# Attention bias moved from VectorE into a TensorE accumulation, and three steps of the layer plan moved one weight unit later

## The chip, the cores and the metric

The kernel runs on one NeuronCore of one Trainium2 chip. The metric is the device time of one execution in microseconds (us). TensorE (PE) does matrix products into PSUM; VectorE (DVE) and ScalarE (ACT) work on SBUF and PSUM; GpSimd (POOL) does some elementwise work; SyncE (SP) issues the loads. Each engine takes its own instructions in order and waits for the others on semaphores.

## What is computed

The reference is a trunk of two equal layers on 256 tokens of width 1024. Each layer mixes tokens in three branches and then runs a SwiGLU feed-forward. The branch that the change touches most is the differential attention (8 heads, two score maps each). Its bias is minus a slope of the head times the distance of query and key:

```python
def block(args):
    qi, start = args
    sc = jnp.einsum('bqhcd,bkhcd->bhcqk', qi, k, preferred_element_type=jnp.float32)
    qpos = start + jnp.arange(Q_BLOCK)
    dist = jnp.abs(qpos[:, None] - kpos[None, :]).astype(jnp.float32)
    sc = sc - slopes[None, :, None, None, None] * dist
    p = jax.nn.softmax(sc, axis=-1)
    attn = p[:, :, 0] - lam * p[:, :, 1]
    return jnp.einsum('bhqk,bkhe->bqhe', attn.astype(v.dtype), v)
...
cb = jnp.einsum('bclgn,bcsgn->bcgls', Cc, Bc)
m = cb[:, :, :, None] * segsum_exp(a)
y_diag = jnp.einsum('bcgrls,bcsgrp->bclgrp', m, xdt)
```

The last three lines belong to the state-space branch (32 heads in 4 groups, 2 chunks of 128 tokens, forwards and backwards); `cb` is the product of its C and B rows. The third branch attends to a memory (4 heads). The branches are gated and projected (`w_branch`, `w_out`).

## The kernel before, in words

**Units.** All weights of a layer are cut into 220 units of 512 KB. Per unit SP loads the raw fp32 weights, ACT casts them to fp32r (`wH`, `split_h`, L818), DVE or POOL subtracts to get the rest (`wL`, `split_l`, L1163 and L1093), and PE multiplies three times (high by high, low by high, high by low), 24 matmuls of 256 columns or 12 of 512. There is a ring of 4 slots. ACT, DVE and SP work 3 units ahead of PE: what these engines do "after unit u" comes behind their part for unit u + 3. Units come in groups of 4 to 11 that share a PSUM pair; after the last unit of a group ACT or DVE empties it.

**Steps.** Everything that is not a unit is a step. `layer_plan` (L107 to L196) writes down after which unit a step stands, and all engines walk the same list in `each_step` (L404): unit, emptying of a finished group, steps. So the order on every engine is fixed, and an engine that waits in a step holds all that stands behind it. In a layer the units are: 26 to 49 the q, k, v projections, 50 to 73 the inputs of the state-space branch (`xbc`), 74 to 89 its gate `z`, 90 to 121 gates and projections of two branches, 122 to 145 gate and projection of the state-space branch, then the output projection and the feed-forward (154 on). The numbers are those of the plan before the change.

**Attention.** A head is four steps. `da_scores`: PE makes both score maps in the side banks S0 and S1; DVE adds the distances times -8 slope while copying to `sc` (L1362), takes the row maximum (L1365) and its negative (L1367); ACT takes the exponential in place with row sums (L954). `da_combine`, two units later: DVE joins the maps (L1371 to L1379). `da_turn`: PE transposes the result into S2 (L695), ACT copies it to `attT` (L959). `da_values`, one unit later: PE multiplies by v, ACT scales and squares (L967, L972). Heads 0 to 3 begin every 3 units (from unit 39), heads 4 to 7 every 4 units (from unit 54). Beside heads 4 to 7 runs the convolution on DVE (`conv`, L1401 and L1407), two steps of about 4.6 us for every 4 units, followed by its silu on ACT (L984) and transposes (`xs_turn`).

**State-space branch.** `cb_diag` after unit 77: DVE multiplies B by C (`cbprod`, L1429), PE sums it in 8 one-column matmuls into S2; `d_gain` (DVE, L1434) uses them. `cb` of group 0 is after unit 77 as well; it needs the last silu. From there a pipeline of 16 ticks runs to unit 123: `rows` (SP loads rows), `diff` (DVE, L1447, L1449), `decay_exp` (ACT, L1014), `decay` (DVE, L1457), `diag` and `off` (PE), `assemble` (DVE, L1467 to L1479), `ssm_norm`, `ssm_out` (PE transposes, L776, then DVE L1492, ACT L1027, DVE L1170). The last four `ssm_out` stand after units 125 to 128; unit 130 on PE waits for the last of them (L1499).

## Time and profile before

| | |
|---|---|
| median of three timed runs | 1583.02 us (1580.55, 1583.02, 1587.58) |
| the profiled execution | 1577.17 us, its span 1575.4 us |
| PE busy | 1437.5 us, 91% of the span |
| DVE busy | 983.2 us, 62% |
| ACT busy | 803.5 us, 51% |
| mean granted TensorE clock | 0.973 |
| chain that ended last | PE 57%, DVE 15%, the sequencer of DVE (DVEq) 9%, ACT 8%, issue 6% |
| read from memory | 252.80 MB, 161 GB/s over the span |

Busy time is the time in which an instruction runs; short matmuls overlap, so a matmul of 512 columns lasts about 0.4 us and the next one starts after 0.23 us. DVEq rows are drains, in which the engine empties its pipeline; they are not counted as busy. The two layers give the same rows some 771 us apart. All times of rows below are in us from the start of the span, durations by group in ns.

### The profile page before, as it was taken

To read this page: it belongs to the slowest core of one execution; us is meant where nothing else is said; L and a number is where in the kernel's file an instruction comes from. 1 tells how busy PE (TensorE), PEld (TensorE's weight loads), DVE (VectorE), ACT (ScalarE), POOL (GpSimd) and SP (SyncE) were. 2 spreads that over 40 slices of the span, in tenths; PEclk is the share of its full clock that TensorE was granted. 3 is DMA by queue.
4 is the path that set the end of the run, shared out by engine and by line. 5 is a ranking of instruction groups with operands and counts; after the bars stand their busy time and mean duration, and the time that the engine had idled before them with its cause. 6 is when DMAs were issued, how large, how long until landed. Compare 5 with 4: busy or idle time off the path is not lost.

```text
span 1575.4 us, 25511 instructions
## 1 busy us (share of the span) xinstructions
PE 1437.5 (91%) x8889; PEld 1280.5 (81%) x8889; DVE 983.2 (62%) x1288; ACT 803.5 (51%) x1151; POOL 338.5 (21%) x162
## 2 busy tenths in 40 slices
PE   5999887969898999999999998886998899999997
PEld 4899787858677779999889987786886677799986
DVE  5445569977787635555432555799677775465544
ACT  4545556746343545444444555675554344454453
POOL 2410000001112144454433000000011113345453
PEclk9999999989999999999999999999899999999999
DMA  5644343455654555656555444335655555565664
GB/s 191 196 144 127 118 121 107 135 149 199 203 150 155 165 172 161 196 168 227 189 170 178 134 124 120 108 110 150 194 190 164 157 161 176 159 187 174 196 215 149
DMA packets 158499, 255.52 MB, mean 162 GB/s; under 512 B 12730, under 2 KB 58924, under 8 KB 158380
## 3 DMA queue, kind: packets, MB, share of 16 engines
q1 hardware_dynamic: 156427, 252.41, 51.6%
q10 hardware_dynamic: 1952, 1.61, 0.3%
q8 instruction: 64, 1.05, 0.3%
q14 instruction: 56, 0.45, 0.1%
HBM read 252.80 MB, written 1.18 MB: 161 GB/s over the span
## 4 chain that ended last, share of the span: by engine, by line
PE 57%; DVE 15%; DVEq 9%; ACT 8%; issue 6%; DMA 2%; ACTq 1%; SPq 0%; POOL 0%; POOLq 0%
PE PS L528 52%; ACT wH L818 4%; DVE wL L1163 4%; PE S L528 4%; DVE regA L1407 3%; DVEq L1404 3%; DMA w_raw<-in_w_branch_dram 2%; DVEq L1448 1%; DVE small L1365 1%; ACT scr L954 1%; DVEq L1364 1%; PE S L535 1%; DVE scr L1449 1%; DMA w_raw<-in_w_in_dram 1%; ACT regA L984 1%
## 5 line engine op out<-in xcount | busy, mean ns | idle before, releaser
L1163 DVE TENSOR_TENSOR wL<-w_raw,wH 128x1024 fp32r<-128x1024 f32 (+1 forms) x330 | 461.3, 1404 | 391.6 <-ACT wH L818 378.1
L818 ACT CAST wH<-w_raw 128x1024 fp32r<-128x1024 f32 (+1 forms) x443 | 455.0, 1041 | 239.9 <-PE PS L528 201.4
L528 PE MATMUL PS<-hH,wH 128*128 128x256 f32 x1472 | 424.6, 288 | 0.0
L528 PE MATMUL PS<-hL,wH 128*128 128x256 f32 x1472 | 418.9, 285 | 0.0
L528 PE MATMUL PS<-hH,wL 128*128 128x256 f32 x1472 | 418.8, 285 | 0.0
L1093 POOL TENSOR_TENSOR wL<-w_raw,wH 128x1024 fp32r<-128x1024 f32 (+1 forms) x113 | 286.0, 2533 | 433.7 <-ACT wH L818 433.6
L528 PEld LDWEIGHTS PS<-hH,wH 128*128 128x128 f32 x1472 | 285.1, 194 | 5.0 <-issue 4.6
L528 PEld LDWEIGHTS PS<-hL,wH 128*128 128x128 f32 x1472 | 285.1, 194 | 0.3
L528 PEld LDWEIGHTS PS<-hH,wL 128*128 128x128 f32 x1472 | 284.7, 193 | 0.0
L528 PE MATMUL PS<-wH,actH 128*128 128x512 f32 x560 | 223.8, 400 | 3.1 <-DVEq L1499 3.1
L528 PE MATMUL PS<-wH,actL 128*128 128x512 f32 x560 | 219.6, 392 | 0.0
L528 PE MATMUL PS<-wL,actH 128*128 128x512 f32 x560 | 219.5, 392 | 0.0
L528 PE MATMUL PS<-wH,hH 128*128 128x512 f32 (+1 forms) x416 | 167.6, 403 | 1.7 <-DVE wL L1163 1.7
L528 PE MATMUL PS<-wL,hH 128*128 128x512 f32 (+1 forms) x416 | 161.8, 389 | 0.0
L528 PE MATMUL PS<-wH,hL 128*128 128x512 f32 (+1 forms) x416 | 161.8, 389 | 0.0
L1109 POOL TENSOR_TENSOR scr<-regA,dts 128x512 f32<-128x512 f32 x16 | 21.7, 1359 | 603.8 <-DVEq L1409 472.4
L528 PEld LDWEIGHTS PS<-wH,actH 128*128 128x128 f32 x560 | 106.2, 190 | 24.8 <-DVEq L1499 3.9
L528 PEld LDWEIGHTS PS<-wL,actH 128*128 128x128 f32 x560 | 106.0, 189 | 22.9
L528 PEld LDWEIGHTS PS<-wH,actL 128*128 128x128 f32 x560 | 106.2, 190 | 20.7
L528 PEld LDWEIGHTS PS<-wH,hH 128*128 128x128 f32 x416 | 81.1, 195 | 19.2 <-DVE wL L1163 3.4
L528 PEld LDWEIGHTS PS<-wL,hH 128*128 128x128 f32 x416 | 80.7, 194 | 16.2
L528 PEld LDWEIGHTS PS<-wH,hL 128*128 128x128 f32 x416 | 80.8, 194 | 14.3
(223 smaller groups left out, 1510.4 us busy)
## 6 DMA issues: line engine op xcount, KB each, us to landing
w_raw<-in_w_in_dram SPq DMA_DIRECT2D x192, 512.0 KB
w_raw<-in_w_ffn_in_dram SPq DMA_DIRECT2D x176, 256.0 KB
w_raw<-in_w_branch_dram SPq DMA_DIRECT2D x64, 512.0 KB
w_raw<-in_w_ffn_out_dram SPq DMA_DIRECT2D x44, 512.0 KB
w_raw<-in_w_mem_kv_dram SPq DMA_DIRECT2D x35, 512.0 KB
scr<-cs_rows SPq DMA_DIRECT2D x64, 256.0 KB, 5.1
w_raw<-in_w_out_dram SPq DMA_DIRECT2D x16, 512.0 KB
regA<-in_mem_dram SPq DMA_DIRECT2D x6, 512.0 KB, 4.8
```

Source lines behind the costliest of these rows:

```text
L528: return nc.tensor.matmul(o, l, r, start=first, stop=last, skip_group_check=True)
L535: ins = nc.tensor.transpose(dst[:, at:at + P], src(t, k), ident[:, :])
L818: nc.scalar.copy(wH[:, slot].rearrange("p k c -> p (k c)")[:, q], raw[:, slot].rearrange("p k c -> p (k c)")[:, q]).then_inc(h_done[slot], 1)
L954: nc.scalar.activation(v, v, ACT.Exp, bias=nmx[b][:, q:q + 1], scale=0.125, accum_out=sm[b][:, q:q + 1])
L984: nc.scalar.activation(cacc[i % 2], cacc[i % 2], ACT.Silu)
L1093: nc.gpsimd.tensor_tensor(wL[:, slot].rearrange("p k c -> p (k c)")[:, q], raw[:, slot].rearrange("p k c -> p (k c)")[:, q], wH[:, slot].r ...
L1109: nc.gpsimd.tensor_tensor(v3(xw, HPG), v3(xsN[:, 1 - c, UC * g:UC * (g + 1)], HPG), wgt[:, q:q + HPG].unsqueeze(2).broadcast_to([P, HPG, DH]),
L1163: v.tensor_tensor(wL[:, slot].rearrange("p k c -> p (k c)")[:, q], raw[:, slot].rearrange("p k c -> p (k c)")[:, q], wH[:, slot].rearrange ...
L1364: dve.drain()
L1365: v.tensor_reduce(mx[b], v3(sc[b], 4), AX.X, ALU.max)
L1404: dve.drain()
L1407: v.scalar_tensor_tensor(cacc[b % 2][:, j, :], cin[:, j, k:k + T], p_cw[:, q:q + 1], cacc[b % 2][:, j, :], ALU.mult, ALU.add)
```

## The change

Four things are changed. (1) The bias: for each map PE first multiplies a constant tile `slopes` (a diagonal of -8 slope, bf16) by `dist` into S0 or S1 (128x512) and then adds the scores onto it. DVE takes the maximum straight from the two banks, one reduction each; the addition L1362 is gone. ACT takes the exponential from the banks into `sc` and now frees them; it also writes the tile for the head after next (`slope_tile`). (2) `da_turn` and `da_values` of every head stand one unit later. (3) `cb_diag` becomes two steps, `cb_prod` on DVE and `cb_diag` on PE a unit later; `d_gain` stands after unit 81 in place of 78. (4) All ticks, with `cb`, `rows`, `ssm_norm` and `ssm_out`, stand one unit later.

```diff
@@ layer_plan
         put(at, "da_scores", h)
         put(at + 2, "da_combine", h)
-        put(at + 3 + (h >= HALF), "da_turn", h)
-        put(at + 4 + (h >= HALF), "da_values", h)
+        put(at + 4 + (h >= HALF), "da_turn", h)
+        put(at + 5 + (h >= HALF), "da_values", h)
...
-    start, per = u + 5, 1.28
-    put(u + 3, "cb_diag", 0)
-    put(u + 4, "d_gain", 0)
+    start, per = u + 6, 1.28
+    put(u + 4, "cb_prod", 0)
+    put(u + 5, "cb_diag", 0)
+    put(u + 7, "d_gain", 0)
@@ PE, da_scores
                         take(lay, m)
+                        if m == 0:
+                            pe.wait_ge(slope_ready, HEADS * lay + i + 1)
+                        mm(S[m][:, :], slopes[:, P * (i % 2):P * (i % 2 + 1)], dist[:, :], True, False)
                         r = slice(DH * m, DH * (m + 1))
                         for t in range(NT):
                             ins = mm(S[m][:, T * t:T * (t + 1)], qT[half][r, j, P * t:P * (t + 1)],
-                                     kT[half][r, j, :], True, True)
+                                     kT[half][r, j, :], False, True)
@@ ACT
+            def slope_tile(i):
+                nc.scalar.activation(slopes[:, P * (i % 2):P * (i % 2 + 1)], ident[:, :], ACT.Copy,
+                                     scale=-8.0 * slope(i)).then_inc(slope_ready, 1)
...
                 elif kind == "da_scores":
                     b = i % 2
+                    if i >= 2:
+                        act.wait_ge(da_turned, HEADS * lay + i - 1)
+                    else:
+                        act.wait_ge(xa_turned, XH * lay + XH)
                     act.wait_ge(da_max, HEADS * lay + i + 1)
                     for q in range(4):
-                        v = sc[b][:, T * q:T * (q + 1)]
-                        nc.scalar.activation(v, v, ACT.Exp, bias=nmx[b][:, q:q + 1], scale=0.125,
-                                             accum_out=sm[b][:, q:q + 1])
+                        ins = nc.scalar.activation(sc[b][:, T * q:T * (q + 1)],
+                                                   S[q // 2][:, T * (q % 2):T * (q % 2 + 1)], ACT.Exp,
+                                                   bias=nmx[b][:, q:q + 1], scale=0.125,
+                                                   accum_out=sm[b][:, q:q + 1])
+                        if q % 2 == 1:
+                            ins.then_inc(side_free[q // 2], 1)
+                    if i + 2 < HEADS:
+                        slope_tile(i + 2)
                     act.drain().then_inc(da_exp, 1)
@@ DVE
                 elif kind == "da_scores":
                     b = i % 2
                     dve.wait_ge(da_sc, HEADS * lay + i + 1)
-                    if i >= 2:
-                        dve.wait_ge(da_turned, HEADS * lay + i - 1)
-                    else:
-                        dve.wait_ge(xa_turned, XH * lay + XH)
                     for m in range(2):
-
-                        v.scalar_tensor_tensor(sc[b][:, 512 * m:512 * (m + 1)], dist[:, :], -8.0 * slope(i),
-                                               S[m][:, :], ALU.mult, ALU.add).then_inc(side_free[m], 1)
-                    dve.drain()
-                    v.tensor_reduce(mx[b], v3(sc[b], 4), AX.X, ALU.max)
+                        v.tensor_reduce(mx[b][:, 2 * m:2 * m + 2], v3(S[m][:, :], 2), AX.X, ALU.max)
                     dve.drain()
...
-                elif kind == "cb_diag":
+                elif kind == "cb_prod":
                     dve.wait_ge(silu_done, 6 * lay + 6)
                     dve.wait_ge(da_yt, 4 * lay + 4)
                     v.tensor_tensor(cbprod, BT, CT, ALU.mult).then_inc(prod_done, 1)
```

The order on ACT around head 1 (`regB<-PS` copies empty groups, `scr<-S` by a COPY is the turned map going to `attT`, the four ACTIVATE are the exponentials). Before:

```order
L818 CAST wH<-w_raw 128x1024
L959 COPY scr<-S 128x512
L951 REGISTER_ALU
L954 ACTIVATE scr,small<-scr,small 128x256 x4
L818 CAST wH<-w_raw 128x1024
L967 ACTIVATE scr<-S,small 128x128 x2
L972 ACTIVATE junk,small<-scr 128x128 x2
```

After (L824 is the cast, L971 the exponentials, L912 the slope tile, L982 the copy of the turned map, L990 and L995 the values):

```order
L824 CAST wH<-w_raw 128x1024
L969 REGISTER_ALU
L971 ACTIVATE scr,small<-S,small 128x256 x4
L912 ACTIVATE slopes<-ident 128x128
L824 CAST wH<-w_raw 128x1024
L982 COPY scr<-S 128x512
L824 CAST wH<-w_raw 128x1024
L990 ACTIVATE scr<-S,small 128x128 x2
L995 ACTIVATE junk,small<-scr 128x128 x2
```

The copy of the turned map of head 0 stood before the exponentials of head 1 and now stands behind them, the slope tile and one more cast.

The order on PE after the last attention transposes (L712), where `onesR,scr` are the one-column sums of `cbprod` and `regA` by `regA` is `cb`. Before:

```order
L712 MATMUL S<-ident,scr 128x128 x4
L524 REGISTER_ALU
L528 MATMUL S<-onesR,scr 128x1 x8
L524 REGISTER_ALU
L749 REGISTER_ALU
L528 MATMUL S<-regA 128x256 x2
L590 REGISTER_ALU
L528 MATMUL PS<-wH,hH 128x512
```

After, with the 12 matmuls of unit 79 ahead of the first row:

```order
L531 MATMUL PS<-wL,hH 128x512
L527 REGISTER_ALU
L531 MATMUL S<-onesR,scr 128x1 x8
L595 REGISTER_ALU
L531 MATMUL PS<-wH,hH 128x512
```

The sums now stand behind units 78 and 79, and `cb` between these two.

On DVE at the same place (L1171 is the low part of the last attention output, L1429 `cbprod`, L1447 and L1449 `diff`). Before:

```order
L1171 SCALAR_TENSOR_TENSOR actL<-S,lp,actH 128x512
L1427 ISA
L1429 TENSOR_TENSOR scr<-regA 128x1024
L1446 REGISTER_ALU
L1447 TENSOR_TENSOR scr<-scr,dts 128x512
```

After:

```order
L1194 SCALAR_TENSOR_TENSOR actL<-S,lp,actH 128x512
L1186 TENSOR_TENSOR wL<-w_raw,wH 128x1024
L1442 ISA
L1444 TENSOR_TENSOR scr<-regA 128x1024
L1461 REGISTER_ALU
L1462 TENSOR_TENSOR scr<-scr,dts 128x512
```

One split of weights more stands ahead of `cbprod` and of `diff`.

## Rows read from the trace of the kernel before

**Rows 1.** Windows: stretch, its length, busy of PE PEld DVE ACT POOL, clock, DMA

```profile
160.00:222.00 62.00, 53.63 (x394) 48.85 (x392) 33.77 (x49) 36.11 (x82) 0.00 (x0) 1.00 0.41 120
222.00:323.00 101.00, 85.47 (x628) 78.67 (x624) 92.80 (x172) 66.47 (x114) 0.00 (x0) 0.97 0.43 125
333.00:340.00 7.00, 6.79 (x24) 6.14 (x25) 1.99 (x4) 1.29 (x2) 0.00 (x0) 0.52 0.38 99
340.00:410.00 70.00, 70.00 (x331) 57.52 (x329) 51.93 (x63) 40.41 (x48) 8.39 (x7) 1.00 0.59 201
410.00:534.00 124.00, 106.78 (x479) 85.12 (x478) 95.54 (x115) 53.33 (x69) 16.02 (x10) 0.94 0.53 158
```

**Rows 2.** Waits of PE, whole span: total us, times, longest

```profile
PE S L695 <- DVEq L1379: 30.5, 14, 4.3
PE S L528 <- DVE scr L1429: 20.6, 2, 10.3
PE S L528 <- DVEq L1471: 19.5, 7, 5.0
```

**Rows 3.** Timeline, head 2 of the first layer: start, duration, engine, what

```profile
184.39 1.14 PE L528 MATMUL S<-regB 64*128 64x256 f32 x8
188.47 0.51 ACT L954 ACTIVATE scr<-scr,small 128x256 f32<-128x256 f32 x1 [3.39 <-DVE small L1367]
193.20 1.99 ACT L818 CAST wH<-w_raw 128x1024 fp32r<-128x1024 f32 x2
195.99 0.88 DVE L1377 SCALAR_TENSOR_TENSOR scr<-scr,small 128x256 f32<-128x256 f32 x2
196.95 0.66 PE L695 MATMUL S<-ident,scr 128*128 128x128 f32 x4 [2.14 <-DVEq L1379]
```

**Rows 4.** Groups of instructions by line and shape: count, busy us, mean ns

```profile
L1362 DVE SCALAR_TENSOR_TENSOR scr<-dist,S 128x512 f32<-128x512 bf16 x32 | 20.5, 682 | 3.6 <-PE S L528 3.0 <-issue 0.6
L1365 DVE TENSOR_REDUCE small<-scr 128x4 f32<-128x1024 f32 x16 | 19.5, 1220 | 1.5
L1338 DVE TENSOR_REDUCE small<-S 128x2 f32<-128x512 f32 x8 | 5.5, 692 | 6.1 <-PE S L528 6.1
L954 ACT ACTIVATE scr<-scr,small 128x256 f32<-128x256 f32 x64 | 31.8, 497 | 47.8 <-DVE small L1367 47.8
L937 ACT ACTIVATE scr<-S,small 128x256 f32<-128x256 f32 x16 | 7.4, 470 | 16.6 <-DVE small L1340 16.6
L972 ACT ACTIVATE junk<-scr 128x128 bf16<-128x128 f32 x32 | 9.6, 302 | 1.4
L528 PE MATMUL S<-scr,cboff 128*128 128x512 f32 x16 | 8.2, 592 | 0.0
```

**Rows 5.** Timeline from the last attention output to unit 78, first layer

```profile
322.24 0.66 PE L712 MATMUL S<-ident,scr 128*128 128x128 f32 x4 [1.65 <-DVE actL L1171]
326.95 1.06 ACT L984 ACTIVATE regA<-regA 128x1024 f32<-128x1024 f32 x1 [9.98 <-DVEq L1409]
331.83 1.23 DVE L1429 TENSOR_TENSOR scr<-regA 128x1024 f32<-128x1024 f32 x1 [0.28 <-issue]
333.21 3.55 PE L528 MATMUL S<-onesR,scr 128*128 128x1 f32 x16 [10.31 <-DVE scr L1429]
338.11 0.99 PE L528 MATMUL PS<-wH,hH 128*128 128x512 f32 x1
```

**Rows 6.** Timeline, last two `ssm_out` and unit 130, first layer

```profile
529.44 0.62 ACT L1027 CAST actH<-scr 128x512 fp32r<-128x512 f32 x1 [1.94 <-DVEq L1494]
532.95 0.62 ACT L1027 CAST actH<-scr 128x512 fp32r<-128x512 f32 x1 [1.94 <-DVEq L1494]
534.38 0.50 PE L528 MATMUL PS<-wH,actH 128*128 128x512 f32 x1 [1.55 <-DVEq L1499]
534.95 0.40 PE L528 MATMUL PS<-wL,actH 128*128 128x512 f32 x1
535.18 0.39 PE L528 MATMUL PS<-wH,actH 128*128 128x512 f32 x1
```

More of the change, by code:

```diff
@@ L242, in build @@
         junk = sb("junk", UC, BF16)
+        slopes = sb("slopes", 2 * P, BF16)
         def v3(ap, n):
@@ L346, in build @@
             "cst_turned", "cst_copied", "cst_stored", "dt_log"))
+        slope_ready = sem("slope_ready")
         prod_done, cbdiag_done, dgain_done = sem("cb_prod"), sem("cb_diag"), sem("d_gain")
@@ L933, in step @@
                 elif kind == "xa_scores":
+                    if i == 0:
+                        slope_tile(0)
+                        slope_tile(1)
                     b = i % 2
```

## The prediction

> **What bounds the kernel now.** I read the table of windows first, then the list of PE's waits, then the timeline at the three places where these waits are. PE is busy 91% of the span, so a change pays only where PE stands still, or where PE's wait is the end of a chain on DVE and ACT that the change makes shorter. The windows [rows 1] show three regimes in the mixing part of a layer. From 160 to 222 (heads 0 to 3) PE is busy 53.6 of 62 us, DVE only 33.8 and ACT 36.1: no engine is full, so the holes in PE are latency. From 222 to 323 (heads 4 to 7 beside the convolution) DVE is busy 92.8 of 101 us, and with its drains full; PE's 85.5 is what DVE lets through. From 340 to 410 PE is busy all the time. (A unit of 12 fp32r matmuls of 512 columns is 2.76 us of PE, 0.23 apart from start to start, 534.95 to 535.18 [rows 6]; the units of 24 with 256 columns take as long.) From 410 to 534 DVE and ACT hand work to each other and PE waits again.
>
> The waits [rows 2] say what PE stood still for: 30.5 us for the joined attention map before its transposes (14 waits in two layers, 7 per layer), 20.6 us for `cbprod` (twice 10.3), and 19.5 us in the ticks for S2 to be freed. The first two are what the change aims at. The second layer repeats the first, so I work out one layer and double it.
>
> **Heads 0 to 3: the turn a unit later.** Head 2 shows the chain [rows 3]: PE begins the scores at 184.39 and ends them at 185.5; DVE adds the bias and takes the maximum, and the exponentials start at 188.47 (four at 0.5, to 190.5); then ACT has two casts and the values of the head before between them, DVE a split of weights behind the second cast, and the join from 195.99 lets the transposes go at 196.95, after a wait of 2.14. The four heads wait 62.0 - 53.6 = 8.4 us together [rows 1]. Moved one unit, the transposes have 2.76 us more of PE work ahead of them, and also the values and scores that used to follow; the chain itself is 1.2 us shorter (next part). The mean wait is 2.1, less than the one unit, so all 8.4 go.
>
> Two things come back. First, the bias costs PE two matmuls of 128x512 per head. No bf16 matmul is in the trace. Below, it is nothing where PE would wait anyway; above, the nearest row is the fp32 one of the same shape, which comes as two instructions of 592 ns that overlap [rows 4], about 1.0 us. I take 0.23, the spacing of the fp32r matmuls of 512 columns [rows 6]. 8 matmuls are 1.8 us (range 0 to 8). The Trainium skill ("TensorE: Matmul & The Clock Gate", section "Back-to-back issue gap") gives about 216 ns for an isolated bf16 matmul of 512 columns and about 131 ns in a sustained stream; by these the 8 would be 1.7 or 1.0 us. No bf16 row here decides it, and the fp32r spacing of 230 ns stands nearer to the first.
>
> Second, a new wait. The copy of the turned map stood before the exponentials of the next head on ACT and now stands behind four exponentials, a slope tile and a cast, while PE reaches the values 2.76 us after the transposes. Counted from the end of the scores: two reductions and the negation 1.6 us, four exponentials and the sums 2.2, the slope tile 0.3 (like the small ACTIVATE of 302 ns [rows 4]), a cast 1.0 [rows 3], and, as estimates from that cast, 0.8 for a copy of half its size with its drain: 5.9 us. PE has a unit, the transposes of 0.66 and a unit, 2.76 + 0.66 + 2.76 = 6.2. That is level; semaphores add a little, and at head 2 the emptying of a group (a copy as large as a cast, 1.0 us) comes between. I take 1.6 us for the four (0 to 5).
>
> Sum on PE: 8.4 - 1.8 - 1.6 = 5.0 us. The norm of the first four heads must now wait for values that come one unit later, with a square root and a table load in front of it, and DVE stands in that norm before the maximum of head 4. I count 0.6 for it, so DVE begins the second half **4.4 us** earlier (1 to 7).
>
> **Heads 4 to 7: DVE is the bound.** Per head two additions of 682 ns go, and one reduction of 1220 ns becomes two of 692, by the reductions of memory attention from PSUM [rows 4]: 1.36 - 0.16 = 1.2 less. Four heads: **4.8 us** (4.2 to 5.5). PE's bias matmuls here lie under DVE, as do ACT's: its exponentials get 27 ns faster each (470 from PSUM against 497 [rows 4]). The turn moved later frees nothing here but PE, which then waits for DVE in another place. The Trainium skill has a rule against this edit ("VectorE: DVE Perf Modes", section "The TRN2 errata"): a PSUM source costs DVE a fixed 120 cycles, an SBUF source 58. For 512 and 1024 elements at its 0.96 GHz that is two times 658 ns in place of 1127, 0.19 us more per head where the rows make it 0.16; by it the four heads would give 4.7 us.
>
> **`cbprod`.** Before [rows 5]: the last attention transposes end at 322.90; PE waits for `cbprod` until 333.21, does the sums (3.55) and `cb` at the half clock (333 to 340 has a granted clock of 0.52 [rows 1], that is 1.2 GHz), and starts unit 78 at 338.11. Two units more, the first partly at the half clock, put unit 80 at 344.6. The stretch from 322.90 is 21.7 us. After, on the same base: unit 78 to 325.7; `cb` waits for the silu, which ends at 328.0 [rows 5], then 1.0; unit 79 to 331.9; the sums wait for `cbprod`. That ended 5.0 us after the silu; one split (1.2) is added ahead of it, so it ends near 334.3. The sums take 1.8 at the full clock: unit 80 at 336.1. That is 8.5 us less, but the ticks now hang on a unit 2.76 later: **5.7 us** for what follows. On DVE the second `diff` gives the same within 0.5. Bounds: if the clock stays low because two shorter waits stand there, 3; if ACT's cast for the split comes early, 8.
>
> **Ticks.** The plan of all ticks moves as one, with SP's `rows` loads between the same weight loads relative to the ticks, and POOL's `scale` and `off` too. The number of table switches on ACT stays. I count nothing. `d_gain`, three units later, is used first by POOL five units on. PE full from 340 to 410 means that an earlier start there is passed on.
>
> **The end of the branch.** The last four `ssm_out` are a loop of DVE and ACT with 3.51 us per turn (529.44 to 532.95 [rows 6]), and unit 130 waits 1.55 for it. All of it now stands behind one more split on DVE, 1.2 us: **-1.3 us** (0 to -2.8; the latter if the loop is paced by PE, a whole unit).
>
> **Sum.** Per layer 4.4 + 4.8 + 5.7 - 1.3 = 13.6 us, two layers 27. From the profiled 1577.2 (span 1575.4 and 1.8 around it) that is 1550. The median of the timed runs, 1583.0, is 5.8 above the profiled execution; I add it: **1556 us**, 1.7% less.
>
> **Rivals.**
>
> *The gain stops at the ticks.* From 340 on the stage is held by DVE and ACT hand-offs and by loads at 201 GB/s [rows 1]. If loads or these hand-offs take back what PE wins before, only what DVE does less stays: 4.8 + 1.2 per layer, 12 us in all, 1571 us. For it: after 410 every PE wait ends on DVE [rows 2]. Against: nothing in the stage is tied to an outside clock, DVE itself arrives earlier, and 125 GB/s before 323 leave the loads slack.
>
> *More than that.* If no new wait comes at the values (+1.6), `cbprod` gives 8 and the 19.5 us of waits for S2 [rows 2] shrink by a quarter because POOL and ACT are further ahead, it is 20 us per layer: 1543 us. For it: the waits shorten the low clock stretches as well (0.94 mean from 410 to 534 [rows 1]). Against: the order inside the ticks is unchanged.
>
> *Slower: the values wait for ACT.* PE waits at `da_values` because the copy is behind the exponentials. It is level by my sum (5.9 against 6.2). It turns the result over if it costs more than 13.6 / 8 = 1.7 us on each of eight heads beyond my count. At 3 us a head (exponentials from PSUM delayed by the maximum, plus an emptied group each time) it is 24 per layer, ten more than the gain: 1583 + 20 = 1603 us. Against: in heads 4 to 7 a wait of PE below DVE's pace is free, so only heads 0 to 3 can pay, 12 us at most; and ACT is busy 36 of 62 us. That makes it unlikely.
>
> A fourth: the bias matmul in another number format could cost 1.0 us each; 8 per layer on PE's path add 6 per layer, 1568 us. It is within the range.
>
> **How the numbers follow.** 0.62 for the forecast (own range 1548 to 1566), 0.18 for the gain that stops at the ticks, 0.12 for more, 0.04 for slower, 0.04 for no change by mishap of parts. The range must leave no more than 0.2 out: 1541 to 1572 takes in most of the first three and the bounds of the terms. A measurement of this kernel tells 0.5% (7.9 us) from no change. Below 1575: nearly all of the first three, less the upper end of the second, 0.88. Within 0.5%: 0.08. Slower: 0.04.
>
> **What would show it.** PE's wait for the join gone in heads 0 to 3 and small in heads 4 to 7; a new small PE wait for ACT's copy at the values, 0 to 1 us; the bias matmuls 0.23 apart; DVE's period per head of 4 units shorter by 1.2; in place of the 10.3 us two waits of about 2.4 at `cb` and at the sums, with the clock full soon after; unit 80 some 18 us earlier than at 344.6 (9 from upstream, 8.5 here); unit 130's wait a little longer. I am wrong if the waits in the ticks grow by what is won before, or if the wait at the values exceeds 2 us a head.

## The result, and the profile after

| | before | changed |
|---|---|---|
| median of the timed runs | 1583.42 us (4 runs, 1580.55 to 1587.58) | 1567.85 us (4 runs, 1562.98 to 1572.21) |
| profiled execution: span, time | 1575.4, 1577.17 | 1561.1, 1562.98 |
| busy PE / DVE / ACT | 1437.5 / 983.2 / 803.5 us (91% of the span for PE) | 1465.0 / 971.7 / 804.8 us (94% for PE) |

The ratio is 0.9907, 95% interval 0.9888 to 0.9925: some 15 us faster. The forecast was 1556, 27 us faster, with a range of 1541 to 1572. The sign, the place and the range were right; about half of the gain is missing.

Windows of the changed kernel, first layer, in the columns of [rows 1] (busy times in the order PE, PEld, DVE, ACT, POOL). The first goes from the scores of head 0 to just after those of head 4, the third from the last attention transposes to the end of the sums of `cbprod`:

```profile
158.00:218.00 60.00, 59.67 (x402) 52.14 (x400) 29.51 (x45) 37.83 (x86) 0.00 (x0) 1.00 0.42 123
218.00:312.00 94.00, 87.17 (x628) 80.01 (x626) 86.11 (x165) 65.57 (x116) 0.00 (x0) 0.98 0.44 129
312.00:326.00 14.00, 10.70 (x46) 8.38 (x47) 12.72 (x19) 7.05 (x8) 1.04 (x1) 0.86 0.39 115
326.00:340.00 14.00, 14.00 (x51) 11.37 (x52) 7.79 (x12) 8.73 (x9) 1.04 (x1) 0.77 0.69 226
394.00:523.00 129.00, 108.87 (x486) 86.84 (x486) 99.53 (x116) 55.86 (x73) 15.05 (x11) 0.93 0.50 155
```

Read the first row against [rows 1]: PE's holes in heads 0 to 3 are gone (59.67 of 60.00 busy, against 53.63 of 62.00), and yet the stretch is only 2 us shorter. PE waited 8.0 us less and worked 6.0 us more. That is one of the missing pieces, and the timeline of head 2 shows it. Behind the row of the scores in [rows 3], the next unit of the kernel before began here:

```profile
185.46 0.50 PE L528 MATMUL PS<-wH,hH 128*128 128x512 f32 x1
```

In the changed kernel:

```profile
179.78 0.39 PE L531 MATMUL S<-dist,slopes 128*128 128x512 bf16 x1
180.10 1.13 PE L531 MATMUL S<-regB 64*128 64x256 f32 x4
181.16 0.39 PE L531 MATMUL S<-dist,slopes 128*128 128x512 bf16 x1
181.49 1.13 PE L531 MATMUL S<-regB 64*128 64x256 f32 x4
182.54 0.50 PE L531 MATMUL PS<-wH,hH 128*128 128x512 f32 x1
```

Before, the eight score matmuls of both maps stood in one row of 1.14 us, and the next unit began 1.07 after their start (184.39 to 185.46). Now four of them, one map, take 1.13 us by themselves (1.06 to the next start), after a bias matmul that takes 0.32 to the next start. The step is 182.54 - 179.78 = 2.76 us, 1.7 longer than before; I had counted 0.46.

The waits of PE over the whole span, which answer to [rows 2]:

```profile
PE S L531 <- DVEq L1486: 25.5, 9, 6.6
PE PS L531 <- DVEq L1514: 8.6, 2, 4.3
PE S L531 <- ACTq L983: 6.7, 4, 3.0
PE S L531 <- ACTq L1008: 4.9, 2, 2.4
PE S L531 <- DVE scr L1444: 1.3, 2, 0.7
```

The 30.5 us for the join are gone, the 20.6 for `cbprod` have become 4.9 for the silu and 1.3 for `cbprod`. What grew: the ticks' wait for S2 (19.5 to 25.5), unit 130's wait (twice 4.3, where [rows 6] has 1.55), and the new wait of the values for ScalarE's copy (twice 0.33 and twice 3.04, L983 is the drain behind that copy).

Groups by line and shape, in the columns of [rows 4]:

```profile
L1380 DVE TENSOR_REDUCE small<-S 128x2 f32<-128x512 f32 x32 | 20.6, 684 | 11.9 <-PE S L531 11.9
L971 ACT ACTIVATE scr<-S,small 128x256 f32<-128x256 f32 x64 | 29.4, 472 | 46.3 <-DVE small L1382 46.3
L912 ACT ACTIVATE slopes<-ident 128x128 bf16<-128x128 f32 x16 | 4.8, 314 | 0.0
```

These are the estimates of the prediction (692, 470, 302 ns) within 4%. The `cb` stretch of the first layer, answering to [rows 5]:

```profile
312.20 0.66 PE L718 MATMUL S<-ident,scr 128*128 128x128 f32 x4 [1.63 <-DVE actL L1194]
318.03 1.50 PE L531 MATMUL S<-regA 128*128 128x256 f32 x4 [2.44 <-ACTq L1008]
324.19 2.38 PE L531 MATMUL S<-onesR,scr 128*128 128x1 f32 x16 [0.66 <-DVE scr L1444]
326.43 0.77 PE L531 MATMUL PS<-wH,hH 128*128 128x512 f32 x1
330.42 0.63 PE L531 MATMUL PS<-wH,hH 128*128 128x512 f32 x1
```

The fourth row starts unit 80, 14.2 us after the transposes; before it was 22.4 (322.24 to 344.60). The 0.63 in the last row (0.40 at the full clock) is TensorE at 1.2 GHz: the granted clock is 0.77 in the window that starts at 326. Unit 79, ahead of the sums, ran at 1.2 GHz in part as well (0.43 a matmul until 321.9).

To split the gain I cut a layer at five places that both traces have: the scores of head 0, the scores of head 4, the last attention transposes, the first `off` that reads `cboff` (the third of the layer; "the first `off`" below) and the first transposes of the feed-forward input (its row with `xN`). Starts in the first layer: 158.97, 221.16, 322.24, 395.37, 598.62 before; 155.50, 215.49, 312.20, 382.81, 590.86 after.

| stretch, first layer | before | changed | gain | forecast |
|---|---|---|---|---|
| heads 0 to 3 | 62.2 | 60.0 | 2.2 | 4.4 |
| head 4 to the last attention output | 101.1 | 96.7 | 4.4 | 4.8 |
| to the first `off` | 73.1 | 70.6 | 2.5 | 5.7 |
| to the feed-forward input | 203.2 | 208.1 | -4.8 | -1.3 |
| sum | 439.7 | 435.4 | 4.3 | 13.6 |

The second layer gives the same within 0.6 (439.1 and 435.2). The two layers account for 8 of the 14.3 us between the spans. The other 6 lie where the change does nothing: 3.4 ahead of the first layer's memory attention and 2.5 between the first layer's feed-forward input and the second layer's head 0 (331.7 and 329.2 us). For the first of these, the same window of before and, in the second fence, of the changed kernel:

```profile
97.00:104.00 7.00, 7.00 (x37) 7.00 (x37) 3.58 (x7) 3.88 (x4) 0.00 (x0) 0.53 0.54 164
```

```profile
97.00:104.00 7.00, 7.00 (x62) 7.00 (x62) 5.05 (x13) 5.90 (x8) 0.00 (x0) 1.00 0.55 153
```

The granted clock (third number from the end) is 0.53 in the one and 1.00 in the other, with no idle time in either. Over the thirteen profiles of this study that attention starts between 105.1 and 109.1 us, and the second stretch takes 329.2 to 335.4; the changed kernel's profile has the lowest of both. So a profile alone can't tell 3 us from nothing. The medians must decide, and the experiments are read by them first.

### The profile page after: what moved, and what is told of

It reads as the page before. It is cut to its first block, busy times and chain, and to the rows that moved or that the text cites. A ratio compares the mean times of both kernels' runs of the same rounds, so it can differ in the third digit from the quotient of the medians.

```text
span 1561.1 us, 25559 instructions
## 1 busy us (share of the span) xinstructions
PE 1465.0 (94%) x8921; PEld 1295.4 (83%) x8921; DVE 971.7 (62%) x1272; ACT 804.8 (52%) x1167; POOL 333.9 (21%) x162
## 4 chain that ended last, share of the span: by engine, by line
PE 63%; DVE 13%; DVEq 9%; issue 6%; ACT 6%; DMA 2%; ACTq 0%; POOL 0%; SPq 0%; POOLq 0%
PE PS L531 56%; PE S L531 5%; DVE wL L1186 3%; DVE regA L1422 3%; DVEq L1419 3%; ACT wH L824 3%; DVEq L1463 2%; PE S L538 1%; DVE scr L1462 1%; DVE scr L1464 1%; DMA w_raw<-in_w_branch_dram 1%; DMA w_raw<-in_w_in_dram 1%; DVEq L1381 1%; ACT regA L1007 1%; DVEq L1476 1%
## 5 line engine op out<-in xcount | busy, mean ns | idle before, releaser
L824 ACT CAST wH<-w_raw 128x1024 fp32r<-128x1024 f32 (+1 forms) x443 | 454.8, 1041 | 241.2 <-PE PS L531 203.4
L531 PE MATMUL PS<-wH,actH 128*128 128x512 f32 x560 | 227.4, 406 | 8.6 <-DVEq L1514 8.6
L1132 POOL TENSOR_TENSOR scr<-regA,dts 128x512 f32<-128x512 f32 x16 | 17.2, 1074 | 567.8 <-DVEq L1424 454.4
L531 PEld LDWEIGHTS PS<-wL,actH 128*128 128x128 f32 x560 | 107.4, 192 | 23.6
```

The source lines that it names most:

```text
L531: return nc.tensor.matmul(o, l, r, start=first, stop=last, skip_group_check=True)
L824: nc.scalar.copy(wH[:, slot].rearrange("p k c -> p (k c)")[:, q], raw[:, slot].rearrange("p k c -> p (k c)")[:, q]).then_inc(h_done[slot], 1)
L1132: nc.gpsimd.tensor_tensor(v3(xw, HPG), v3(xsN[:, 1 - c, UC * g:UC * (g + 1)], HPG), wgt[:, q:q + HPG].unsqueeze(2).broadcast_to([P, HPG, DH]),
```

## The experiments

Ratios are to the kernel before, timed beside them. Where two kernels have the same plan in a stretch, their traces still differ by up to 3 us there, by where the clock falls; numbers by stretch are of the first layer.

### The parts alone

`e_bias_only` takes the changed kernel with the plan of before:

```
-        put(at + 4 + (h >= HALF), "da_turn", h)
-        put(at + 5 + (h >= HALF), "da_values", h)
+        put(at + 3 + (h >= HALF), "da_turn", h)
+        put(at + 4 + (h >= HALF), "da_values", h)
...
-    start, per = u + 6, 1.28
-    put(u + 4, "cb_prod", 0)
-    put(u + 5, "cb_diag", 0)
-    put(u + 7, "d_gain", 0)
+    start, per = u + 5, 1.28
+    put(u + 3, "cb_diag", 0)
+    put(u + 4, "d_gain", 0)
```

> The bias goes to TensorE, but the plan stays that of the kernel before (turns, values, cb_prod, cb_diag, d_gain and ticks where they were). Theory A (the terms of the prediction with the score step as measured, 1.6 us longer on TensorE): heads 0 to 3 TensorE still waits for the join, the chain is 1.2 us shorter and TensorE's step 1.6 longer, so these heads give -2 to +1 us; heads 4 to 7 give 1.2 us each on VectorE, 4.8 a layer: 3 to 5 us a layer, 1583 -> 1573 to 1577. Theory B (the stage of heads 4 to 7 is held by the join's chain and not by VectorE's sum): 1581 to 1586, with waits for the join larger than the 4.3 us at their worst before.

Measured 1582.9 us, ratio 1.0004 (0.9986 to 1.0021): nothing. VectorE is 1.2 us a head lighter and the waits for the join fell:

```profile
PE S L700 <- DVEq L1393: 18.7, 12, 3.4
```

from the 30.5 of [rows 2], 11.8 us, but the score steps grew by 16 x 1.7 = 27 us on the same engine. Theory A misses by 6 us: its 4.8 us for heads 4 to 7 did not show (101.2 us, as before). Theory B has the number but not the reason, since the waits for the join shrank. What is left is that TensorE's longer step eats the gain in all eight heads; `e_bias_pair` below tests that.

`e_turn_only` is the kernel before with the first two plan lines as changed.

> The kernel before with da_turn and da_values one unit later in the plan, bias still on VectorE, cb and ticks as before. Theory A (holes in TensorE in heads 0 to 3 are latency): the 8.4 us of waits a layer go, 1 to 3 come back as waits of the values for ScalarE's copy, heads 4 to 7 unchanged: 5 to 7 us a layer, 1583 -> 1569 to 1573. Theory B (VectorE's later stage absorbs it, since second half begins with its backlog): the waits go but VectorE reaches the last heads no earlier: 1580 to 1584.

Measured 1575.3 us, ratio 0.9959 (0.9942 to 0.9976): 7 us, between the theories. Heads 0 to 3 gave 3.9 us (62.2 to 58.3; 2.3 in the second layer), the later heads nothing. The waits for the join are gone, but with the bias on VectorE ScalarE's copy comes later than in the changed kernel. Heads 0 and 4 in the timeline:

```profile
178.12 1.13 PE L528 MATMUL S<-regB,scr 128*128 128x128 f32 x8 [2.26 <-ACTq L960]
247.25 2.04 PE L528 MATMUL S<-regB,scr 128*128 128x128 f32 x8 [4.44 <-ACTq L960]
```

Twelve such waits make 27.5 us. So the slower rival's mechanism exists; it is the shorter chain of the bias part that keeps it small in the changed kernel (6.7 us).

`e_cb_only` is the kernel before with the other half of the plan (and `cb_prod` as a step of its own on DVE).

> The kernel before with only cb_prod, cb_diag, d_gain and the ticks later. Theory A: from the last attention transposes to unit 80 the stretch falls from 22.4 to about 14.5 us, of which 2.8 go back because the ticks hang on a later unit, 2 to 3 to a half-clock stretch at the start of the ticks and 2 to 3 to a longer wait at unit 130: 0 to 3 us a layer, 1583 -> 1577 to 1583. Theory B (this part gives its full 5.7 us a layer, and the gain is lost in the heads): 1572.

Measured 1584.5 us, ratio 1.0023 (1.0008 to 1.0038): a loss of 2 us, just past the end of theory A; theory B is out. To the first `off` it wins 4.1 us (73.1 to 69.0), and from there it loses 6.1 (203.2 to 209.3). Its largest piece is in PE's waits:

```profile
PE PS L529 <- DVEq L1500: 8.6, 2, 4.3
```

Unit 130 waits 4.3 us in each layer; before it is 1.55 [rows 6]. The wait grew by 2.75, the length of a unit. In the second layer the stretch behind the first `off` lost 7.2.

`e_plan_only` has both halves of the plan, without the bias on TensorE.

> The kernel before with both plan parts (turn and values later; cb_prod, cb_diag, d_gain and ticks later), bias still on VectorE. Theory A (the two parts act in different stages and add): -7.3 us (turn alone) + 1.9 (cb alone) = 1577. Theory B (they work together: a head start won in the heads is kept only if the ticks do not stand behind cb_prod): 1568 to 1572, and the bias on TensorE then gives the changed kernel nothing at all or costs.

Measured 1576.7 us, ratio 0.9961 (0.9947 to 0.9975): theory A, the two halves add. So bias alone 0, plan alone 6, both 15. In the traces of this kernel and of the changed one heads 0 to 3 take the same (59.8 and 60.0); what the bias adds to the plan lies in heads 4 to 7 (102.3 and 96.7). The bias part and the turn need each other. With the turn and no bias the wait for ScalarE's copy is 25.5 us, in the changed kernel 6.7. That the later turn in its place leaves TensorE the room for its longer score step is what `e_pair` and `e_bias_pair` below bear out.

### The score step

`e_pair` on the changed kernel:

```
                     for m in range(2):
                         take(lay, m)
                         if m == 0:
                             pe.wait_ge(slope_ready, HEADS * lay + i + 1)
                         mm(S[m][:, :], slopes[:, P * (i % 2):P * (i % 2 + 1)], dist[:, :], True, False)
+                    for m in range(2):
                         r = slice(DH * m, DH * (m + 1))
                         for t in range(NT):
```

> Edit on the changed kernel: on TensorE the two bias matmuls of a head come first, then the score matmuls of both maps next to each other, as they stood in the kernel before. Theory A (the bias matmul, which uses all 128 rows, stands between two maps that use rows 0 to 63 and 64 to 127 and overlapped in the kernel before, 1.14 us for both): the score step goes from 2.75 us to about 0.31 + 0.31 + 1.14 = 1.76 us; in heads 0 to 3 TensorE has no waits in the changed kernel, so 4 x 1.0 us a layer come off, 8 us in all, 1568 -> 1560; in heads 4 to 7 VectorE is the bound and nothing comes. Theory B (matmuls that accumulate on the bias are slow by themselves, 1.13 us per map wherever they stand): step and time unchanged, 1568.

Measured 1560.0 us, ratio 0.9870 (0.9849 to 0.9891), 8 us below the changed kernel; the two intervals just touch, the traces decide. Head 2 in the timeline:

```profile
179.09 0.61 PE L531 MATMUL S<-dist,slopes 128*128 128x512 bf16 x2
179.62 1.14 PE L531 MATMUL S<-regB 64*128 64x256 f32 x8
180.69 0.50 PE L531 MATMUL PS<-wH,hH 128*128 128x512 f32 x1
```

The step is 1.60 us instead of 2.76, heads 0 to 3 take 55.4 us instead of 60.0 (4 x 1.16 = 4.6), and heads 4 to 7 are unchanged at 96.7. Theory A, in size and place. The two bias matmuls start 0.23 apart, as forecast; the 0.32 is the way to an fp32 matmul behind one of them. The single records, which the row above merges, show the overlap itself: the eight score matmuls start in four pairs, 0.01 us apart in a pair and 0.22 to 0.32 from pair to pair, as they do in the kernel before.

The traces differ in one more place. From the last attention transposes to the first `off` the changed kernel takes 70.6 us in both layers and `e_pair` 67.4, with the same plan and the same two waits. After the sums the clock stays full here (granted clock 1.00):

```profile
323.00:337.00 14.00, 14.00 (x68) 11.71 (x68) 10.82 (x16) 9.95 (x10) 1.05 (x1) 1.00 0.77 249
```

The other kernels with this part of the plan take 67.4 to 70.6 there. So the low clock behind the sums comes in some of the traces and not in others. Between the two layers this profile is 5.6 us longer than that of the changed kernel (334.8 and 329.2), so the spans do not settle what the 3.2 us a layer are worth.

That adjacency is what counts does not yet say why. `e_same_half` keeps the order of `e_pair` and lets both maps read the same rows of the array (map 1's own rows are left out):

```
-                        r = slice(DH * m, DH * (m + 1))
+                        r = slice(0, DH)
```

> The paired form, but both maps read rows 0 to 63 of the queries and keys (map 1's own rows are left out of the computation). Adjacency, shapes and number of matmuls are those of the paired form. Theory A (two matmuls of 64 rows run side by side only when they use different row halves of the array): the two maps take 1.13 each again, the score step grows from 1.67 to about 2.8 us and the time from 1560 to 1567, that of the changed kernel. Theory B (the step is short because the bias matmuls no longer alternate with the scores, whatever rows they use): step 1.67, 1560.

Measured 1566.9 us, ratio 0.9909 (0.9887 to 0.9932), the changed kernel's time. Head 2:

```profile
182.94 0.38 PE L531 MATMUL S<-dist,slopes 128*128 128x512 bf16 x1
183.25 1.99 PE L531 MATMUL S<-regB 64*128 64x256 f32 x8
185.17 0.50 PE L531 MATMUL PS<-wH,hH 128*128 128x512 f32 x1
```

(The record of one bias matmul is missing ahead of these.) The eight score matmuls need 1.92 us from start to start where they needed 1.07, and heads 0 to 3 take 58.8 us where they took 55.4; 0.85 x 8 heads is 6.8 us, and the time rose by 6.9. Theory A in kind; its 2.8 for the step was a little too much. The two maps run side by side in different row halves, and not in the same one. The Trainium skill says this of the array ("TensorE: Matmul & The Clock Gate", "The mechanism" under "Packing small matmuls — row/col tiling"): matmuls in different row groups overlap. The trace agrees for two fp32 matmuls of 64 rows (1.07 us against 1.92). In the changed kernel a matmul of all 128 rows stands between the maps, and the overlap is lost, 1.16 us a head. Whether one of 64 rows there would cost the same was not tried.

`e_bias_pair` puts the paired form into the plan of before (`e_bias_only` with the edit of `e_pair`).

> The bias on TensorE with both bias matmuls first and the maps adjacent, plan of the kernel before. The form with a bias matmul between the maps gave 1582.9, no gain, though VectorE has 1.2 us a head less to do. Theory A (the 1.7 us a head that TensorE's score step grew by ate it in all eight heads, since the joins keep TensorE and VectorE in step there): the step shrinks by 1.15 us, 8 heads: 4 to 9 us a layer, 1583 -> 1566 to 1575. Theory B (only heads 0 to 3 see TensorE's step, heads 4 to 7 are VectorE's and gain nothing from either): 4 x 1.15 a layer, 1574 at best, with the stretch from scores 4 to values 7 at 79.7 us as before. Theory C (the waits for the join take it back): 1580 to 1583.

Measured 1565.2 us, ratio 0.9884 (0.9866 to 0.9902), 18 us below `e_bias_only`, 1 us better than theory A's best. Heads 0 to 3 fell from 63.2 to 58.7 us and heads 4 to the last output from 101.2 to 96.9: the 4.3 us that VectorE's lighter work is worth in heads 4 to 7, which `e_bias_only` had hidden. Theory B is out, its 79.7 us between the scores of head 4 and the values of head 7 became 75.3. So in the plan of before TensorE's step counts in all eight heads, through the join; with the later turn only in heads 0 to 3 (`e_pair`: 96.7 in heads 4 to 7 in either order).

### The wait at the values

`e_copy_first` is `e_pair` with ScalarE's copy of heads 4 to 6 ahead of the next head's exponentials:

```
         at = u + (1 + 3 * h if h < HALF else 4 * h)
+        if h > HALF:
+            put(at, "da_copy", h - 1)
         put(at, "da_scores", h)
...
-                elif kind == "da_turn":
+                elif kind == "da_copy" or kind == "da_turn" and (i < HALF or i == HEADS - 1):
```

> The paired form of the changed kernel, and ScalarE copies the turned map of heads 4 to 6 ahead of the exponentials of the next head (in the paired form it waited behind them, and TensorE stood 3.19 us at the values of head 4 and 1.56 us at head 6 in each layer). Theory A (heads 4 to 7 are paced by VectorE, 91% busy there; a wait of TensorE below that pace is free): the two waits vanish and waits for weight splits or joins take their place; 1560 -> 1557 to 1561. Theory B (the waits stand on the path): 4.7 us a layer, 1560 -> 1551.

Measured 1560.7 us, ratio 0.9852 (0.9834 to 0.9870), against 1560.0: theory A. The wait for the copy fell from 10.2 us (6 times) in `e_pair` to this:

```profile
PE S L533 <- ACTq L986: 0.7, 2, 0.4
PE PS L533 <- DVE wL L1189: 10.7, 8, 1.9
```

In its place PE waits for weight splits (9.5 in `e_pair`), for ScalarE's `regA` copies (11.2 us, 6 times) and 1.4 us a layer more for `cbprod`; the stretch is as long as it was (96.5 and 96.7 us). The longest new wait of the changed kernel stands below VectorE's pace and costs nothing; this was tried on the paired form.

### The ticks

`e_pair_ticks` is `e_pair` with the ticks where they were before:

```
-    start, per = u + 6, 1.28
+    start, per = u + 5, 1.28
     put(u + 4, "cb_prod", 0)
     put(u + 5, "cb_diag", 0)
-    put(u + 7, "d_gain", 0)
+    put(u + 6, "d_gain", 0)
...
-        put(start + int(per * 8 * g) - 2, "cb", g)
+        put(start + int(per * 8 * g) - (2 if g else 1), "cb", g)
```

> The paired form of the changed kernel with all ticks one unit earlier (where they were in the kernel before), cb_prod and the first cb of group 0 where the change has them, cb_diag likewise, d_gain one unit earlier. Theory A (moving the ticks later costs a unit at the end of the branch, where unit 130 waits 4.3 us for the last ssm_out instead of 1.55): unit 130's wait returns to about 1.5, 2.7 us a layer, and the wait of 6.6 us for S2 near 464 changes: 1560 -> 1553 to 1556. Theory B (the ticks an unit earlier make TensorE wait as much more at cb and the first diag, since they hang on the silu of the last convolution): 1558 to 1562.

Measured 1548.3 us, ratio 0.9779 (0.9761 to 0.9797), 12 us below `e_pair`, twice what theory A gave. Unit 130 and the sums of `cbprod` in its timeline:

```profile
323.94 2.00 PE L531 MATMUL S<-onesR,scr 128*128 128x1 f32 x16 [2.96 <-DVE scr L1445]
...
516.26 0.50 PE L531 MATMUL PS<-wH,actH 128*128 128x512 f32 x1 [1.57 <-DVEq L1515]
```

The wait at unit 130 is back at 1.57, and the first matmul there takes 0.50 and not 0.80: the clock no longer falls behind it. From the first `off` to the feed-forward input it is 202.2 us, against 210.1 in `e_pair` and 203.2 before (second layer: 202.8, 207.7, 202.7). Up to the first `off` it costs 1.2 us (68.6 against 67.4; 2.8 in the second layer), with a wait of 2.96 for the sums. The move of the ticks had taken back more than the later `cb_prod` gave.

`e_sums_late` adds one thing to it: the sums one unit later (`cb_diag` at u + 6, `d_gain` at u + 7).

> The paired form with the ticks one unit earlier (1548.3), and on top of that the sums of cb_prod on TensorE one unit later (and d_gain a unit later, behind them). TensorE waited 2.96 us a layer there for cb_prod, which VectorE reaches behind the first diff. Theory A (the wait stands on TensorE's path and nothing else needs the sums before the first scale): 2.8 us a layer, 1548 -> 1543. Theory B (the first diag or the weight splits hold TensorE instead): 1547 to 1549.

Measured 1544.9 us, ratio 0.9768 (0.9748 to 0.9789): 3.4 us below `e_pair_ticks`, between the theories. Its trace has the gain that theory A wants, up to the first `off` (68.6 to 65.8; the other layer 70.1 to 64.5):

```profile
325.90 1.92 PE L531 MATMUL S<-onesR,scr 128*128 128x1 f32 x16 [0.18 <-DVE scr L1445]
```

In the second layer 3.2 of it go again in the ticks. By the ratios, each to its own runs of the kernel before, it is 1.7 us and not 3.4. The intervals of the two ratios overlap, so that it beats `e_pair_ticks` is likely and not shown. It is the fastest version of the study, 1.5% below the changed kernel and 2.3% below the one before.

`e_start4` goes the other way from `e_pair_ticks`: all ticks one unit earlier still (start at u + 4, first `cb` left at u + 4).

> The paired form with the ticks two units earlier than in the change (one earlier than in the kernel before), the first cb where the change has it, cb_diag as in the change. Theory A (each unit that the ticks come earlier takes a unit off the wait of unit 130, until that is gone): 1.55 us a layer less than with one unit, 1548 -> 1545. Theory B (the first diff, decay and diag now reach VectorE before the last silu is out, and TensorE waits for cb_prod and the first diag): 1548 to 1556.

Measured 1551.3 us, ratio 0.9805 (0.9785 to 0.9826), 3 us above `e_pair_ticks` (the intervals overlap, so that it is slower is likely and not shown): theory B's result. Unit 130 waits no more, but the ticks are then 4 to 6 us longer (208.6 and 206.6 to the feed-forward input, 202.2 and 202.8 with one unit), with 23.6 us of waits for S2 against 20.0. Which link in them is late I did not settle.

## Why the prediction was half right

**Heads 0 to 3, 4.4 forecast, 2.2 in the trace.** The step that failed is "the bias costs PE two matmuls of 128x512 per head ... 8 matmuls are 1.8 us". The matmuls themselves were nearly right (0.32 us each to the next start, for 0.23; 0.23 when two stand together). What I left out is what they do to their neighbours: [rows 3] showed `x8` in 1.14 us, eight fp32 matmuls of 64x256 in the time that four take alone, and that row says that the two maps overlap. The diff puts a matmul of all 128 rows between them. It cost 1.16 us a head, 4.6 us a layer and some 8 us of the time (`e_pair`; `e_same_half` gives 7 for the halves alone). All the 8.4 us of waits did go, and the wait at the values in these heads was 0.33, less than the 1.6 I allowed; with the maps together these heads gave 6.8, more than forecast.

**Heads 4 to 7, 4.8 forecast, 4.4 in the trace.** Right in size, and right in cause: `e_bias_pair` shows 4.2 (101.1 to 96.9) from the bias alone. "PE's bias matmuls here lie under DVE" holds as well: 1.16 us a head less of them changes nothing here (`e_pair`). What I missed is on what it hangs. I wrote that the later turn "frees nothing here but PE"; with the plan of before the long score step eats the whole gain (`e_bias_only`), so that freedom is what lets the gain through.

**`cbprod`, 5.7 forecast, 2.5 to the first `off`.** The stretch to unit 80 lost 8.1 us as worked out (8.5), and the wait for the silu came as said (2.44). The wait for the sums was 0.66 and not 2.4: `cbprod` was ready when forecast, but unit 79 ahead of it had lost 1.4 us to the half clock. The sums took 2.24 for the 1.8 "at the full clock", and the clock was down behind them: unit 80 and the start of 81 ran at 1.2 GHz (326.43 to 332, 0.43 a matmul for 0.23), some 2.7 us more. I had this as the bound of 3, "if the clock stays low because two shorter waits stand there", and it was that bound that came in this profile. In `e_pair` the clock was full again behind the sums and the whole 5.7 came (73.1 to 67.4), so the 2.5 is not a fixed price of the change. Unit 80 began 18.2 us earlier than before, as the signs had it, "9 from upstream, 8.5 here"; that is in part luck, since 3.5 of it come from ahead of head 0 and only 6.6 from the heads.

**Ticks and end, -1.3 forecast, -4.8 in the trace.** This is the largest error, and it was in the step "I count nothing" for the ticks and in the value taken for the end. The windows of this stretch, before and changed:

```profile
395.30:598.60 203.30, 183.49 (x829) 148.10 (x829) 136.25 (x149) 85.14 (x104) 42.53 (x22) 0.97 0.55 171
```

```profile
382.80:590.80 208.00, 185.03 (x817) 149.24 (x816) 137.62 (x147) 83.78 (x102) 40.06 (x22) 0.94 0.53 164
```

PE stands still 3.2 us longer (19.8 to 23.0) and its work takes 1.5 longer, at a granted clock of 0.94 for 0.97. Of the two ends for unit 130, 0 and -2.8 ("a whole unit"), the far one was true: it waits 4.30 instead of 1.55.

```profile
523.45 0.79 PE L531 MATMUL PS<-wH,actH 128*128 128x512 f32 x1 [4.30 <-DVEq L1514]
```

The last `ssm_out` stand a unit later in the plan and unit 130 does not, so the unit of delay shows in full. The 0.79 shows what follows: TensorE is at the half clock behind that wait, for eight matmuls, 1.6 us that the 2.75 do not contain. `e_cb_only` and `e_pair_ticks` show both from two sides: moving the ticks later loses 6 us in this stretch (7 in the second layer), moving them back wins 8 (5 in the second). The waits for S2 grew by 3.5 us in this stretch of the first layer (9.4 to 12.9), other small waits shrank by 3. The longest wait for S2 is here, with DVE, POOL and PE in one timeline:

```profile
456.96 2.34 POOL L1163 TENSOR_TENSOR regB<-regB,scr 128x1024 f32<-128x1024 f32 x1 [16.64 <-DVEq L1279]
457.05 4.25 DVE L1462 TENSOR_TENSOR scr<-scr,dts 128x512 f32<-128x512 f32 x2 [0.21 <-issue]
459.55 1.20 POOL L1132 TENSOR_TENSOR scr<-regA,dts 128x512 f32<-128x512 f32 x1 [0.25 <-issue]
...
463.88 0.47 PE L531 MATMUL S<-regA,scr 128*128 128x64 f32 x1 [6.57 <-DVEq L1486]
```

The two subtractions of a `diff` take 1.29 us together at 366 and 379 in the same trace; here, beside two instructions of GpSimd, 4.25 (2.80 and 1.52). The Trainium skill ("GPSIMD Engine Reference", "Key points") says that GpSimd shares its SBUF interfaces with VectorE, with contention where VectorE has two inputs in SBUF; this row has two, and agrees. With no GpSimd instruction beside it none of these subtractions takes more than 0.69 us, in any of the thirteen traces. It is the later ticks that bring the two together: a subtraction of 2.80 to 2.82 us stands in both layers of all six kernels whose ticks are later, and in none of the other seven, where the longest is 1.53. So the later ticks cost VectorE 3.0 us a layer at this place; how much of it is in the length of the stretch was not tried by itself.

**The rivals.** "The gain stops at the ticks" (1571) was in part true in its mechanism: the ticks took back 4.8 of 9.1 us a layer, though because they had been moved (`e_pair_ticks`), and no wait of PE in this stretch ends on a load. "The values wait for ACT" happens (3.04 at head 4) and costs nothing (`e_copy_first`). "The bias matmul in another number format" was priced at 1.0 us each and gave 1568, the measured time. That is luck. The extra per matmul came to 0.84, but by the lost overlap and not by the format, and the rest of the missing gain lies in the clock behind the sums and in the ticks.

**The sum.** By the trace 4.3 a layer and not 13.6. Of the 14.3 us between the spans 6 lie outside these stages, where the thirteen profiles vary by as much with the same code. How the 15 us between the medians spread over the stages stays open; the profile of the kernel before was 6 us faster than the median of its runs, and the changed one's 5. That the time came out inside the range is in part luck: with the 8 us of the two layers alone it would be 1575, outside.

## What to carry to other kernels

Before you put a cheap instruction between others, read whether those others overlap: a group that takes no longer than half of it alone is running two at a time, and the price of the insertion is the overlap and not the instruction. When work that ends in a fixed unit of another stream is moved later, price its end first: a step in a plan that is late by a unit cost a whole unit there (unit 130, 2.75 us), however much was gained at its start. And a part that measures zero alone (the bias) can be the one that makes another pay, so take parts out of the whole as well as adding them one by one.

## What the runs showed of the hardware

- Two fp32 matmuls of 64x256 ran side by side in row halves 0 to 63 and 64 to 127: eight in 1.07 us from start to start, 1.92 if all use the same half, and 1.06 for the four of one map behind a matmul of all 128 rows.
- A bf16 matmul of 128x512 took 0.32 us to the start of the fp32 matmul behind it, and a pair of them 0.53.
- At the end of the ticks a wait of 4.30 us was followed by the half clock in both layers of all six kernels that have it (the first matmul took 0.67 to 0.80 us). A wait of 1.53 to 1.57 at the same place was not, in both layers of the six kernels that have that one (0.49 or 0.50).
- Behind the sums of `cbprod`, where TensorE waits 2.44 us at `cb` and 0.66 at the sums one unit later, the same plan ran at the half clock in the changed kernel (granted clock 0.77 in 14 us) and at the full clock in `e_pair` (1.00).
- A VectorE subtraction of 128x512 with both inputs in SBUF took up to 0.69 us alone, up to 1.53 beside a GpSimd instruction of the same size, and 2.80 to 2.82 beside one of 128x1024 that had begun just before it.
